# The gated recurrence of the first layer: exponents of block sums at every level replaced by keys and queries rescaled from level to level, with the gate product in k-tiles between heads

## The reference, cut to what matters

```
f = lb + (1 - lb) * sigmoid(f_logit);  log_f = log(max(f, 1e-6));  key = 1 - f
cum = cumsum(log_f) in the chunk
w = exp(cum[t] - cum[s]) for s <= t, else 0
scores = sum_c qn[t,c] * kn[s,c] * w[t,s,c]
out = scores @ vn + (qn * exp(cum)) @ state
new_state = exp(last) * state + (kn * exp(last - cum)).T @ vn
```

## Time and profile before

| | |
|---|---|
| median of 3 runs | 3363.87 us (3363.17 to 3366.28) |
| the profiled execution | 3358.75 us, span 3356.6 us |
| busy share of the span: PE, DVE, ACT, POOL | 96%, 48%, 32%, 10% |
| granted TensorE clock, mean | 0.98 of full speed |
| PE share of the chain that ended last | 90% (line 409 alone 80%) |

### The profile page before, as it was taken

The page is one execution under the profiler, slowest core; times in us unless marked ns, Lnnn a source line. Parts: engine busy times, 40 slices in busy tenths (PEclk is TensorE's granted clock), DMA queues, the critical chain, the costliest instruction groups (busy, mean ns, idle before and its releaser), DMA issues.

```text
span 3356.6 us, 38850 instructions
## 1 busy us (share of the span) xinstructions
PE 3220.8 (96%) x15546; PEld 2652.5 (79%) x15546; DVE 1618.3 (48%) x1917; ACT 1085.7 (32%) x1157; POOL 322.1 (10%) x178
## 2 busy tenths in 40 slices
PE   6986899999999899999999999999999999999999
PEld 5865698888888789888888777888888777888887
DVE  5365454555334644555534755444433674454433
ACT  2223233444322333444423332233322332233232
POOL 1003110011000001001100200101100120011000
PEclk9998899999999999999999999999999999999999
DMA  3410131222332123122233212222232212222223
GB/s 138 127 46 30 38 144 45 88 99 88 113 126 76 51 74 128 38 98 90 100 112 91 81 63 88 88 101 93 95 106 103 77 63 88 88 88 100 100 100 113
DMA packets 47578, 299.94 MB, mean 89 GB/s; under 512 B 7075, under 2 KB 7331, under 8 KB 13012
## 3 DMA queue, kind: packets, MB, share of 16 engines
q1 hardware_dynamic: 42336, 288.01, 24.3%
q10 hardware_dynamic: 5108, 10.02, 1.3%
HBM read 293.26 MB, written 4.75 MB: 89 GB/s over the span
## 4 chain that ended last, share of the span: by engine, by line
PE 90%; DVE 5%; ACT 2%; issue 1%; POOL 1%; DMA 0%; another core or an unknown queue 0%; ACTq 0%; DVEq 0%; SPq 0%; POOLq 0%
PE G L409 80%; PE psS L869 1%; PE G L876 1%; PE psS L681 1%; DVE wL L1342 1%; PE psT L901 1%; PE psT L490 1%; ACT wH L982 1%; PE psS L465 1%; PE psS L768 1%; PE G L775 1%; DVE mxt L1532 1%; PE psS L462 0%; DMA x<-in_x 0%; DVE ws L1814 0%
## 5 line engine op out<-in xcount | busy, mean ns | idle before, releaser
L409 PE MATMUL G<-hH,wH 128*128 128x512 f32 x2624 | 1042.3, 397 | 11.0 <-DVE wL L1342 5.9
L409 PE MATMUL G<-hH,wL 128*128 128x512 f32 x2624 | 1027.5, 392 | 2.1 <-issue 2.1
L409 PE MATMUL G<-hL,wH 128*128 128x512 f32 x2624 | 1027.7, 392 | 0.0
L1342 DVE TENSOR_TENSOR wL<-raw,wH 128x2048 fp32r<-128x2048 f32 x266 | 647.7, 2435 | 673.3 <-ACT wH L982 673.0
L409 PE MATMUL G<-wsr,wH 128*128 128x512 f32 (+1 forms) x2400 | 713.9, 381 | 14.3 <-DVE ws L2031 9.7
L982 ACT ACTIVATE wH<-raw 128x2048 fp32r<-128x2048 f32 x266 | 506.8, 1905 | 456.0 <-PE G L409 441.5
L409 PEld LDWEIGHTS G<-hH,wH 128*128 128x128 f32 x2624 | 497.6, 190 | 121.0 <-issue 16.4
L409 PEld LDWEIGHTS G<-hH,wL 128*128 128x128 f32 x2624 | 496.3, 189 | 108.3 <-issue 2.5
L409 PEld LDWEIGHTS G<-hL,wH 128*128 128x128 f32 x2624 | 496.7, 189 | 103.4 <-issue 2.4
L409 PEld LDWEIGHTS G<-wsr,wH 128*128 128x128 f32 x2400 | 445.4, 190 | 101.3 <-DVE ws L2031 10.6
L409 PE MATMUL G<-wsr,wL 128*128 128x512 f32 (+1 forms) x1200 | 456.2, 380 | 0.0
(11 more groups left out here) (259 smaller groups left out, 2769.6 us busy)
## 6 DMA issues: line engine op xcount, KB each, us to landing
raw<-in_units SPq DMA_DIRECT2D x266, 1024.0 KB, 4.8
ws<-bias_rows SPq DMA_DIRECT2D x2, 1536.0 KB, 14.8
bias_rows<-ws ACTq DMA_DIRECT2D x1, 2560.0 KB
x<-in_x SPq DMA_DIRECT2D x4, 512.0 KB, 8.2
ws<-in_mem ACTq DMA_DIRECT2D x2, 1024.0 KB, 4.9
ws<-bias_rows ACTq DMA_DIRECT2D x1, 2048.0 KB, 8.4
out_x<-x SPq DMA_DIRECT2D x4, 512.0 KB, 7.6
ws<-in_decay ACTq DMA_DIRECT2D x1, 1280.0 KB, 13.0
```

What stands on the lines that cost most here:

```text
L409: mm = pe.matmul(o, mv if swap else wt, wt if swap else mv, start=first and n == 0, stop=last and n == 2)
L1342: V.tensor_tensor(wL[:, g.p, :], raw[:, g.p, :], wH[:, g.p, :].bitcast(F32), ALU.subtract)\
```

## The change

The running sums now restart every 4 tokens. Keys and queries are scaled once by exponents of them (level 0), kept in KEY and ZA, and from level to level DVE multiplies half of each by the decay of the neighbouring block (`grow`), which POOL forms as products of pairs (five small tables in slot SD+2). ACT takes the exponents once, four heads by two, and the sums of each block of 4 once. PE takes each head as soon as its `grow` is there, and behind every second head one k-tile (6 matmuls) of a gate unit, 16 in all, in place of the two whole units. ACT copies the scores of levels 6 and 7, and stores the two gate jobs behind level 3's end and behind level 7.

```diff
-HG_CHUNK = 64
+HG_BLOCK = 4
-    reset = np.tile((np.arange(S) % HG_CHUNK != 0).astype(np.float64), (P, 1))
+    reset = np.tile((np.arange(S) % HG_BLOCK != 0).astype(np.float64), (P, 1))
+        sums = {4: ws[:, RST, :].rearrange("p (h n) -> p h n", h=4)}
+        for half in (8, 16, 32, 64, 128):
+            n = S // half
+            sums[half] = ws[:, SD + 2, at:at + 4 * n].rearrange("p (h n) -> p h n", h=4)
...
 (PE)                for lev in range(8):
-                        pe.wait_ge(hz_ready, lev + 1)
                         for h in range(4):
                             n = lev * 4 + h
-                            wait(pe, hm_ready, n - 1)
+                            pe.wait_ge(hz_ready, n + 1)
+                            if n >= 26:
+                                pe.wait_ge(hc_ready, n - 25)
+                            else:
+                                wait(pe, hm_ready, n - 1)
...
-                        if lev in (1, 3):
-                            plain(h_op)
+                            if h % 2 == 1:
+                                k = n // 2 % KT
+                                if k == 0:
+                                    take_unit()
+                                    take_job()
+                                for t in range(2):
+                                    w0 = k * 256 + t * P
+                                    mm = passes(G[:, c.job.p * 2 + t, :], w0, w0 + P, h_op, k, slice(0, S),
+                                                k == 0, k == KT - 1)
+                                if k == KT - 1:
+                                    end_job(mm)
+                                    c.unit.off += 1
-                    pe.wait_ge(hm_ready, 32)
+                    pe.wait_ge(hm_ready, 24)
+                    pe.wait_ge(hc_ready, 8)
...
 (ACT)
+                    act.wait_ge(scan_ready, 1)
+                    activation(ws[:, RST, :], flat(CUM, 4).rearrange("p (n l) -> p n l", l=4)[:, :, 3], ACT.Exp)\
+                        .then_inc(t4_ready, 1)
+                    act.wait_ge(tn_ready, c.nrm.v + 4)
+                    for h in range(4):
+                        activation(ws[:, ZA + h, :], ws[:, CUM + h, :], ACT.Exp)
+                        activation(ws[:, ZB + h, :], ws[:, CUM + h, :], ACT.Exp, scale=-1.0).then_inc(he_exp, 1)
+                    step()
+                    step(store(ws[:, GG:GG + 2, :], ACT.Silu))
+                    for n in range(24, 32):
+                        act.wait_ge(hs_done, n + 1)
+                        (copy psS to hsx1 or SX2) .then_inc(hc_ready, 1)
+                    step(store(ws[:, GG + 2:GG + 4, :], ACT.Silu))
...
 (DVE)               step(inputs(0))
+                    for h in range(4):
+                        dve.wait_ge(he_exp, h + 1)
+                        V.tensor_tensor(ZA[h], ZA[h], GQ[h], ALU.mult)
+                        V.tensor_tensor(ZB[h], ZB[h], KEY[h], ALU.mult).then_inc(hz_ready, 1)
+                    dve.wait_ge(t4_ready, 1)
+                    for h in range(4):
+                        dve.wait_ge(hz_ready, h + 1)
+                        V.tensor_tensor(KEY[h], ZB[h], sums[4] of h, each over 4 tokens, ALU.mult).then_inc(hz_ready, 1)
+                    step(inputs(1))
+                    def grow(h, half):
+                        k0, q1 = blocks(ws[:, KEY + h, :], half)[0], blocks(ws[:, ZA + h, :], half)[1]
+                        f0, f1 = even and odd entries of sums[half]
+                        (half 128: one block of each)
+                        V.tensor_tensor(k0, k0, f1.to_broadcast([P, n, half]), ALU.mult)
+                        V.tensor_tensor(q1, q1, f0.to_broadcast([P, n, half]), ALU.mult).then_inc(hz_ready, 1)
+                    for lev in range(7):
+                        for h in range(4):
+                            n = lev * 4 + h
+                            dve.wait_ge(hs_done, n + 1)
+                            if lev > 0:
+                                if h == 0 and lev > 1:
+                                    dve.wait_ge(tb_ready, lev - 1)
+                                dve.wait_ge(hz_ready, n + 1)
+                                grow(h, 2 ** (lev + 1))
+                            if lev < 6:
+                                (mask of the head as before; hm_ready)
+                        if lev == 5:
+                            step(None, act_too=True)
+                    step(None, act_too=True)
...
 (POOL)          pool.wait_ge(tn_ready, c.nrm.v + 4)
+                pool.wait_ge(t4_ready, 1)
+                for i, half in enumerate((8, 16, 32, 64, 128)):
+                    if i:
+                        pool.wait_ge(tb_ready, i)
+                    pair = sums[half // 2].rearrange("p h (n two) -> p h n two", two=2)
+                    W.tensor_tensor(sums[half], pair[:, :, :, 0], pair[:, :, :, 1], ALU.mult).then_inc(tb_ready, 1)
```

More of the change, by code:

```diff
@@ L314, in program @@
         ln_in, ln_ready, scan_ready = sem("ln_in"), sem("ln_ready"), sem("scan_ready")
-        he_in, he_exp, hz_ready, hs_done, hm_ready = (sem("he_in"), sem("he_exp"), sem("hz_ready"),
-                                                      sem("hs_done"), sem("hm_ready"))
+        he_exp, hz_ready, hs_done, hm_ready, hc_ready = (sem("he_exp"), sem("hz_ready"), sem("hs_done"),
+                                                         sem("hm_ready"), sem("hc_ready"))
+        t4_ready, tb_ready = sem("t4_ready"), sem("tb_ready")
         b33_in, b33_mask = sem("b33_in"), sem("b33_mask")
@@ L1159, in _ @@
                     step()
[L1161 to L1169, removed]
-                        else:
[L1172 to L1177, removed]
+                    act.wait_ge(scan_ready, 1)
[9 more added lines that the diff above has]
+                        act.wait_ge(hs_done, n + 1)
+                        b, h = psS[:, n % 2, :], n % 4
+                        if n < 28:
+                            ins = activation(hsx1[:, h], b.rearrange("p (k q) -> p k q", q=P)[:, 0:2, :], ACT.Copy)
+                        else:
+                            ins = activation(ws[:, SX2 + h, :], b, ACT.Copy)
+                        ins.then_inc(hc_ready, 1)
+                    step(store(ws[:, GG + 2:GG + 4, :], ACT.Silu))
                     heads(h_tiles[0:4], src=lambda k: ws[:, RO + k, :])
@@ L1737, in _ @@
                     step(inputs(0))
-                    gq, key = flat(GQ, 4), flat(KEY, 4)
-                    def mask(lev):
+                    for h in range(4):
+                        dve.wait_ge(he_exp, h + 1)
+                        V.tensor_tensor(ws[:, ZA + h, :], ws[:, ZA + h, :], ws[:, GQ + h, :], ALU.mult)
+                        V.tensor_tensor(ws[:, ZB + h, :], ws[:, ZB + h, :], ws[:, KEY + h, :], ALU.mult)\
+                            .then_inc(hz_ready, 1)
+                    dve.wait_ge(t4_ready, 1)
+                    for h in range(4):
+                        dve.wait_ge(hz_ready, h + 1)
+                        V.tensor_tensor(ws[:, KEY + h, :].rearrange("p (n l) -> p n l", l=4),
+                                        ws[:, ZB + h, :].rearrange("p (n l) -> p n l", l=4),
+                                        sums[4][:, h, :].unsqueeze(2).to_broadcast([P, S // 4, 4]), ALU.mult)\
+                            .then_inc(hz_ready, 1)
+                    step(inputs(1))
+                    def grow(h, half):
+                        k0, q1 = blocks(ws[:, KEY + h, :], half)[0], blocks(ws[:, ZA + h, :], half)[1]
+                        pair = sums[half][:, h, :].rearrange("p (n two) -> p n two", two=2)
+                        f0, f1 = pair[:, :, 0:1], pair[:, :, 1:2]
+                        n = S // (2 * half)
+                        if half == 128:
+                            k0, q1, f0, f1, n = k0[:, 0:1, :], q1[:, 1:2, :], f0[:, 1:2, :], f1[:, 0:1, :], 1
+                        V.tensor_tensor(k0, k0, f1.to_broadcast([P, n, half]), ALU.mult)
+                        V.tensor_tensor(q1, q1, f0.to_broadcast([P, n, half]), ALU.mult).then_inc(hz_ready, 1)
+                    for lev in range(7):
                         for h in range(4):
@@ L1743, in mask @@
                             dve.wait_ge(hs_done, n + 1)
[L1744 to L1763, removed]
-                            step(None, act_too=True)
[L1765 to L1775, removed]
@@ L1776, in _ @@
-                    mask(7)
+                            if lev > 0:
[4 more added lines that the diff above has]
+                            if lev < 6:
+                                b = psS[:, n % 2, :].rearrange("p (k q) -> p k q", q=P)
+                                d = ws[:, DD + h, :].rearrange("p (k q) -> p k q", q=P)
+                                if lev == 0:
+                                    ins = V.tensor_tensor(d, b, hmask[:, 0:1, :].to_broadcast([P, 4, P]), ALU.mult)
+                                else:
+                                    wait(dve, hm_ready, n - 3)
```

(6 more changed lines are left out.)

8 lines of the change are left out of this document (4 added, 4 removed).

## The result

In the first timing the changed kernel took 3303.68 us (median of four executions, 3301.23 to 3306.63) beside 3363.52 for the kernel before: ratio 0.9824, 95% interval 0.9807 to 0.9841. Timed again in two more comparisons it stood at 3302.63 and 3299.81 us, and the kernel before at 3357.98 and 3357.39: ratios 0.9845 (0.9825 to 0.9864) and 0.9835 (0.9812 to 0.9858). One execution of the kernel before took 4654 us at a mean granted clock of 0.649 and is left out of these figures. The profiled execution took 3306.63 us, 52.1 less than the one of before.

The account below looks back on a forecast made before the run. PE idles while POOL, ACT and DVE pass four-head blocks through the first layer's recurrence. Levels: 9.5 + 2.2 + 32.65 + 4.53 + 6.21 = 55.1 us instead of 102.1; 3363.87 - 47.0 = 3316.9 us, range 3309 to 3333.

Parts of the forecast that it names:

- The base: Whole kernel: 47.0 us off the profiled 3358.75 gives 3311.7; the shown median's 5.1 us distance is kept, giving 3316.9.
- The start: Entry to level 0: POOL stretches DVE's first split by 1.0 (bounds 0 and 2.5); PE waits 3.0 us for the first mask.
- The clock: Behind PE's wait in level 0: one fall of the granted clock, charged at 2.2 us.
- Levels 1 to 5: First layer's recurrence: PE sets the pace at 6.53 us a level, 32.65 in all.
- The split behind level 5: DVE's split of the next unit, 2.28 us ahead of level 6's grows: covered, by 1.5 us.
- DVE: Levels 1 to 5: two 128x256 products and a mask cost 1.3 us a head overlapped, 1.59 if not.
- the slow-broadcast rival: DVE products in levels 1 to 5: repeated-factor broadcasts far slower; at 2.0 us a product, 13 us slower, 3377; chance 0.04.
- the first rival: Levels 1 to 5: DVE sets the pace, 2.0 to 2.4 us a head, 7.4 to 15.8 us more, 3324 to 3333; chance 0.25.
- The clock rival: All levels: PE's clock stays at 0.50, levels take 93 us, time about 3355; chance 0.04.
- Behind the levels: After level 7: hL ends about 9.3 us later, covered by 4 before POOL's power at 13.7; costed at nothing.

Follow-up runs that it names:

- the barrier kernel: Changed kernel, but PE waits at a level's first head for the products of all four heads, no more at each head: 3311.89 and 3306.00 us in two runs.

## Why the prediction was wrong

Direction and mechanism were right. The step that failed is the last one, "and I keep that distance": the base carried 5.1 us that do not belong to the kernel. The gain was also summed too small, by 2.1 us in the levels, and one term of 3.5 us was not in it. From 3316.9 to 3303.7 are 13.2 us:

- **The base, the largest part.** The text kept the distance of 5.1 us between the profiled execution and the median shown, as if it belonged to the kernel. The executions of the kernel before spread over 16 us in the first comparison; the three shown were all near the top, and later medians of the kernel before are 3357.3 to 3358.0, 6 us lower. Profile against profile the error is 5.1 us (3306.63 against 3311.7), and a range moved down by the same 5.1 (from 3303.9) would have held that; the other 8.1 lie between profile and median, +5.1 before and -3.0 after. The range was built from the costs alone and had no term for this.
- **The start.** The step was "I take 1.0" for POOL in the first split, and 0.64 for each product. The split took 2.28 us, so the bound of 0 was right, but not because POOL did little: POOL's third product stood for the length of the split, as the rows above show, where before it was the split that stood behind L2129. Keys and products came 0.60 to 0.62 apart. The first mask began at 247.37, not 248.7, and PE waited 1.93 us, not 3.0. The order on DVE that the text named, the masks behind the two splits, is what moving the second split behind the masks took away.
- **The clock.** One fall of 2.2 us was charged. In the first profile it came and cost 1.8 (2.56 + 2.44 for what takes 1.78 + 1.39 elsewhere); in the two later ones it did not, and the levels took 51.3 and 51.2. That it is charged at all is a choice that the runs leave open.
- **Levels 1 to 5.** 6.34 us each, not 6.53: a pair of heads is 1.78, by 0.89 as in L695's rows, where I had used 0.95. Level 6 gave 0.4 back: its heads are short, and it wanted the bank of level 5's last head while DVE was still on that head's products, a wait that the text had overlooked. The split behind level 5 was covered, as forecast.
- **DVE.** 1.31 us a head as forecast (a level of four is 5.2, where the text had 5.4). The Trainium skill's "VectorE: DVE Perf Modes" ("The DRAIN you can't avoid") has the next operation wait for an empty pipeline, and adds that one that is not held starts earlier. The trace does not agree with the wait: 128x256 products reported at 0.42 us start 0.34 apart. The broadcast of one factor over 4 to 128 tokens costs nothing extra (0.42, as the plain product in the earlier trace rows), so the slow-broadcast rival falls. One more product a head (1.64 us) shows where the first rival would begin.
- **The clock rival** (the second of the list, called the third in the working) falls: 1.00 from 254 to 306. "TensorE: Matmul & The Clock Gate" of the Trainium skill ("A second HAM failure mode: psum-queue depth-cycling") tells of short idles between groups that make it swing; at the hand-overs between score matmuls and k-tiles nothing of the kind was seen. The wait of 1.93 us was followed by a fall in one of the changed kernel's three profiles.
- **Behind the levels.** hL ended 10.0 us behind them and was covered, as forecast. Yet POOL's power came 14.9 us behind instead of 13.7: the statistics took 3.42 us, with the granted clock at 0.63 and then 0.50, where they had taken 1.96. This fall was not in the sum: 1.2 us lost.
- **Not in the sum at all:** the stall of 2.07 us near 2568 and the fall behind it, 3.5 us, gone because PE's code moved: the barrier kernel, which differs from the changed one in PE's waits alone, stands still again.

47.0 + 2.1 (levels) - 1.2 (behind them) + 3.5 (the stall) + 0.7 (elsewhere) = 52.1, the difference of the profiles.

## What to carry to other kernels

When four engines pass a level's work along in whole blocks, shorten the passing first: here rescaling by a small table in place of sums, exponents and products took off 37 of the 49 us, and filling the gaps with small pieces of independent product work 12 more, but the same filling on the old chain took off under 3. Put long work of no urgency (here a split of 2.3 us) behind the short steps that free a buffer. And before a forecast is made against a median of three, ask how far executions of one program lie apart, and let the range hold that spread. And when a wait in a profile is put down to the engine that finished last, see in another run whether the instruction needs it at all.

## What the runs showed of the hardware

- Executions of one program of 3.3 ms spread over 19 us (75 of the kernel before: 3349.0 to 3367.7), and the time goes with the mean granted clock: 0.981 or 0.982 in every one up to 3356.5, 0.973 to 0.975 in every one from 3363.2 on. The falls of the clock come in the same few places, but not in all of them each time: behind the first wait of the levels in two of eight profiles with k-tiles.
- A stall of PE of 0 to 3.29 us at one place of a loop, behind no semaphore that these runs show it to need, changes with the number of PE's instructions ahead of it (old code with 0, 12, 24, 48 redundant waits: 1.66 to 2.07, 2.58, 3.29, none).
- DVE beside POOL: where both worked on SBUF operands one of them stood, and it was the one that began later. A DVE operation of 128x2048 that takes 2.28 us alone took 4.78 when begun inside a POOL operation of 128x2048, and ended 2.16 us behind it. Begun between two of POOL's small ones it took 2.28, and POOL's next, of 64 elements, took 2.23. At 299.00, begun ahead of POOL's first 128x512 on hL, it took 2.29, and POOL's took 2.86 where its last took 1.27.
